# Hybrid encoder layer on one core: down weights of the short sequence split on GpSimd from the raw array instead of reloaded, loads reordered, a projection placed ahead of the first gates

## The reference

```python
proj = x @ w_in + b_in                                   # D_MODEL 1024 -> 7168
u_lru, g_lru, q, k, v, gate_lru, gate_attn = jnp.split(proj, SPLIT_IDX, axis=-1)
u = depthwise_conv(u_lru, w_lru_conv, b_lru_conv, LRU_CONV_PAD)
h_fwd = rg_lru_scan(u, ...)                              # gates: block-diagonal linear, 8 blocks of 160
h_bwd = flip(rg_lru_scan(flip(u), ...))
y_lru = ((h_fwd + h_bwd) * gelu(g_lru)) @ w_lru_out
attn = windowed_gqa(q, k, v, rel_table, attn_sink)       # keys within +-128
y_attn = attn @ w_attn_out
mix = (sigmoid(gate_lru) * y_lru + sigmoid(gate_attn) * y_attn) @ w_o + b_o
x = layer_norm(ALPHA * x + mix, ln1_g, ln1_b)
hu = depthwise_conv(x @ w_up + b_up, w_ffn_conv, b_ffn_conv, FFN_CONV_PAD)
val, gt = jnp.split(hu, 2, axis=-1)                      # D_FF 3072 each
ffn = (gelu(gt) * val) @ w_down + b_down
return layer_norm(ALPHA * x + ffn, ln2_g, ln2_b)
```

## Time and profile before

| | us |
|---|---|
| median of 3 runs | 2699.28 |
| lowest, highest | 2697.11, 2702.12 |
| the profiled execution | 2699.09 |
| span of its trace | 2697.2 |
| PE busy in it | 2608.7 |
| DVE, ACT, POOL busy | 1596.1, 956.7, 571.0 |

### The profile page before, as it was taken

How to read it: one execution, slowest core, us unless ns; L and a number is a source line. 1 busy time by engine, 2 the same in 40 slices (tenths; PEclk the granted TensorE clock), 3 DMA queues, 4 the chain that set the end, 5 groups by cost and what they waited for, 6 DMA issues and landing times.

```text
span 2697.2 us, 32662 instructions
## 1 busy us (share of the span) xinstructions
PE 2608.7 (97%) x11634; PEld 2150.2 (80%) x11634; DVE 1596.1 (59%) x2037; ACT 956.7 (35%) x1344; POOL 571.0 (21%) x306
## 2 busy tenths in 40 slices
PE   8999999999999999999999999989999999999998
PEld 6787888888788877788888778877788777888886
DVE  7799754334513658888888476457642424644445
ACT  3566713303400025444444333349732312111112
POOL 3554532232133612232322022300000000000000
PEclk9999999999999999999999999999999999999999
DMA  6555554544696843545354899966656783555554
GB/s 219 199 195 178 192 184 154 185 146 163 222 357 239 297 152 133 176 151 186 141 187 148 306 364 337 322 223 219 230 188 226 264 339 126 191 196 195 194 196 163
DMA packets 199872, 571.81 MB, mean 212 GB/s; under 512 B 16167, under 2 KB 43047, under 8 KB 197712
## 3 DMA queue, kind: packets, MB, share of 16 engines
q1 hardware_dynamic: 143712, 469.75, 48.4%
q10 hardware_dynamic: 56048, 100.59, 10.5%
HBM read 338.25 MB, written 223.10 MB: 208 GB/s over the span
## 4 chain that ended last, share of the span: by engine, by line
PE 81%; DVE 9%; DMA 5%; ACT 2%; issue 1%; ACTq 1%; POOL 0%; SPq 0%; DVEq 0%; POOLq 0%
PE ps L1177 35%; PE ps L1569 14%; PE ps L1345 9%; PE ps L1631 5%; PE ps L1519 5%; PE ps L1439 4%; PE ps L1227 3%; PE ps L1328 2%; PE ps L1378 2%; DMA gate_in<-gate_dram 1%; PE ps L1365 1%; PE ps L1230 1%; DMA Hd<-h_dram 1%; DMA W<-w_split 1%; DMA rest_raw<-w_up 1%
## 5 line engine op out<-in xcount | busy, mean ns | idle before, releaser
L1177 PE MATMUL ps<-XH,W 128*128 128x512 f32 x2752 | 812.1, 393 | 26.4 <-DVE XL L2371 11.8
L1177 PEld LDWEIGHTS ps<-XH,W 128*128 128x128 f32 x2752 | 519.3, 189 | 145.3 <-issue 19.1
L1177 PE MATMUL ps<-XL,W 128*128 128x512 f32 x1376 | 483.9, 391 | 0.0
L1177 PEld LDWEIGHTS ps<-XL,W 128*128 128x128 f32 x1376 | 260.3, 189 | 54.1
L1631 PE MATMUL ps<-Wd,Hd 128*128 128x512 f32 x1152 | 265.0, 392 | 8.4 <-DVE Hd L2883 8.4
L1631 PEld LDWEIGHTS ps<-Wd,Hd 128*128 128x128 f32 x1152 | 217.7, 189 | 55.6 <-DVE Hd L2883 10.2
L1345 PE MATMUL ps<-XH,W 128*128 128x512 f32 x672 | 216.4, 393 | 0.0
L1035 POOL TENSOR_SCALAR W<-raw 128x1024 fp32r<-128x1024 f32 (+2 forms) x72 | 90.3, 1254 | 563.1 <-PE ps L1177 302.5
L1036 POOL TENSOR_TENSOR W<-raw,W 128x1024 fp32r<-128x1024 f32 (+2 forms) x72 | 203.1, 2821 | 6.0
L1123 POOL TENSOR_TENSOR A<-raw,A 128x512 fp32r<-128x512 f32 x66 | 127.8, 1936 | 311.9 <-ACT A L2124 305.4
L1569 PE MATMUL ps<-XH,A 128*128 128x512 f32 x528 | 172.5, 394 | 4.9 <-ACT l_e L2148 2.6
(11 more groups left out here) (304 smaller groups left out, 4625.6 us busy)
## 6 DMA issues: line engine op xcount, KB each, us to landing
W<-w_split SPq DMA_DIRECT2D x130, 1024.0 KB, 6.6
w_split<-W SPq DMA_DIRECT2D x59, 1024.0 KB, 6.1
w_split<-A SPq DMA_DIRECT2D x66, 512.0 KB, 3.8
raw<-w_up SPq DMA_DIRECT2D x48, 512.0 KB, 5.8
raw<-w_down SPq DMA_DIRECT2D x48, 512.0 KB, 6.0
w_split<-Wd SPq DMA_DIRECT2D x24, 1024.0 KB, 7.6
raw<-w_qkv_mix SPq DMA_DIRECT2D x28, 512.0 KB, 4.0
h_dram<-l_h SPq DMA_DIRECT2D x24, 512.0 KB, 3.9
```

The source lines that it names most:

```text
L1177: last = nc.tensor.matmul(bank(group, c), lhs(wl, k), rhs(xl, k, c), start=(k == 0 and n == 0), stop=(k == nk - 1 and n == 2))
```

## The change

- **Short MLP.** The four down slabs of a group are no longer fetched as pairs. SP loads the raw slab from `w_down` (512 KB) into `raw[0]` and `raw[1]` by turns, POOL splits it into the slot, and PE waits for POOL (`rest_split`). A load into a buffer waits until the slab two before it is split. The loads stand behind the group's eight fetches in SP's order.
- **Long MLP, down product.** `save_down` and its 24 stores are gone, with the waits on them. The normed rows are loaded on every second step from step 4 to 18, the five bias and norm rows one at a time (steps 5, 6, 7, 13, 15), and the short sequence's x at steps 30 to 36, its heads at 38 to 45. DVE's adding of the normed rows moves accordingly.
- **Long MLP, start of the seven-product scheme.** ACT does `first_product(0, 0)` ahead of `plain_pair(1)`; DVE does `value_third(0, 0)` ahead of the last sums of pair 1; SP loads the raw slabs of the pair after that before it stores the forms.
- **lru, both sequences.** `("g", 0, 0)` stands ahead of `("gates", 0, 0)`, ACT takes its gelu before the gates, and in block 0 the own-channel matmuls of the first two (long) or four (short) groups are issued ahead of the wait for `u_stack`. The wait on `out_stored[1]` moves from before the first `u` to before that gelu.
- **Start.** x comes in parts of 1, 2, 3 and 2 slices, `cols` after all of x, and SP holds the second weight slab back until the second part of x is in, the third until all is.

```diff
-                     ("gates", 0, 0), ("g", 0, 0), ("u", 0, 2), ("g", 0, REST_TILE),
+                     ("g", 0, 0), ("gates", 0, 0), ("u", 0, 2), ("g", 0, REST_TILE),
...
+        X_PARTS = (0, 1, 3, 6, KD)
...
+                    if n in (1, 2):
+                        sp.wait_ge(x_landed[2 * n - 1], 16)
...
-                next_pair(2, 1, up_slab(3, 0))
+                sp.wait_ge(a_split, 6)
+                sp.wait_ge(form_added, 8)
+                load_pair(2 + PLAIN)
+                save_forms(1, 1, up_slab(3, 0))
+                store_h(1)
...
-                def save_down(s, slot, slab):
-                    sp.wait_ge(step_split, s + 1)
-                    sp.dma_start(w_split[slab, :, :, 0:D_MODEL], W_down[slot][:, :, :].bitcast(F32)).then_inc(w_saved[slot], 16)
...
-                    if s % 2 == 0:
-                        save_down(s - 2, (s - 2) % RING, down_slab(s - 2))
-                    else:
+                    if s % 2:
                         next_rest((s - RING) // 2)
...
+                def load_short_down(kk, g=0):
+                    if isinstance(g, int) and g == 0 and kk < 2:
+                        sp.wait_ge(out_stored[kk], 16 * out_count(0)[kk])
+                    else:
+                        sp.wait_ge(rest_split, FAST + FG * g + kk - 1)
+                    sp.dma_start(raw[kk % 2][:, 0:D_MODEL], A["w_down"][FG * g + kk, :, :]).then_inc(raw_in[kk % 2], 16)
+
-                for n in range(12):
+                for n in range(2 * FG):
...
                 with sp.Fori(0, NG - 1) as i:
-                    for n in range(12):
+                    for n in range(2 * FG):
                         fetch(s0 + 12 * i + n + 12 + 3 - slot_user(n), FIRST["mlp"] + 12 * i + n + 12, SLOT[n])
+                    for kk in range(FG):
+                        load_short_down(kk, i + 1)
...
+                with order.loop(NG, FG) as g:
+                    for kk in range(FG):
+                        k, n, slot = kk % 2, 2 * FG + kk, DOWN_SLOT[kk]
+                        pool.wait_ge(raw_in[k], 16 * RAW_SHORT + 32 * g + 16 * (kk // 2 + 1))
+                        pool.wait_ge(slab_done, s0 + 12 * g + n + 3 - slot_user(n))
+                        pool.sem_inc(begun, 1)
+                        order(pool.tensor_scalar(half(1, slot, 0)[:, 0:D_MODEL], raw[k][:, 0:D_MODEL], 1.0, 1.0, ALU.mult, ALU.mult))
+                        pool.tensor_tensor(half(1, slot, 1)[:, 0:D_MODEL], raw[k][:, 0:D_MODEL],
+                                           half(1, slot, 0)[:, 0:D_MODEL].bitcast(F32), ALU.subtract).then_inc(rest_split, 1)
...
+                        ahead = gate_banks(T) if blk == 0 else 0
+                        for place_of, m in enumerate(GATE_ORDER[0:ahead]):
+                            own_block(place_of, m)
+                        if q:
+                            pe.wait_ge(stack_in, 16 * (BLOCKS + blk + 1))
+                        pe.wait_ge(stack_moved[q], 48 * (blk + 1))
+                        for place_of, m in enumerate(GATE_ORDER + (4,)):
+                            if place_of >= ahead:
+                                own_block(place_of, m)
+                            rest_rows(place_of, m)
...
+                        first_product(0, 0)
                         plain_pair(1)
                         gate_centre(1)
                         value_centre(1)
-                        first_product(0, 0)
...
+                            if s == 5:
+                                act.wait_ge(h_ready, FT)
+                                act.wait_ge(h_stored, 16 * FT)
+                            if s % 2 == 0 and s < 4 + 2 * nt:
+                                load_normed((s - 4) // 2)
+                            if s in rows:
+                                dst, name, landed_rows = rows[s]
+                                act.dma_start(dst[:, :], A[name].partition_broadcast(P)).then_inc(landed_rows[0], 16)
...
+                                if s % 2 == 0 and s < FT + 6 + KD:
+                                    load_x(1, (s - FT - 6) // 2, (s - FT - 6) // 2 + 1)
+                                if FT + 14 <= s < FT + 14 + KD:
+                                    head_of_x(1, s - FT - 14)
```

More of the change, by code:

```diff
@@ L123 @@
         for _i in range(_n):
+            if _phase == "mlp" and _i % 12 >= 2 * FG:
+                continue
             _slot = slot_of(_q, _phase, _i)
@@ L131, in use @@
 def use(q, phase, n, g=0):
[L133 removed]
+    return USE[q][phase, n] + (UP_SLOT.count(SLOT[n]) * g if phase == "mlp" else 0)
 PLAIN = 2
@@ L1158, in _ @@
                 pool.sem_inc(cleared, 1)
+                s0 = first_slab(1, "mlp")
+                with order.loop(NG, FG) as g:
+                    for kk in range(FG):
+                        k, n, slot = kk % 2, 2 * FG + kk, DOWN_SLOT[kk]
[5 more added lines that the diff above has]
+                                           half(1, slot, 0)[:, 0:D_MODEL].bitcast(F32), ALU.subtract).then_inc(rest_split, 1)
+                        pool.wait_ge(rest_split, FAST + FG * g + kk + 1)
             @block.tensor
@@ L1184, in slab_in @@
                         pe.wait_ge(split_done, first_slab(q, phase) + n + 3)
+                    elif phase == "mlp" and n >= 2 * FG:
+                        pe.wait_ge(rest_split, FAST + FG * g + n - 2 * FG + 1)
                     else:
@@ L1211, in gates, with own_block @@
                         slab_in(q, "lru", n)
-                        if q:
-                            pe.wait_ge(stack_in, 16 * (BLOCKS + blk + 1))
-                        pe.wait_ge(u_split[q], channel_at[(h, jj)] + 1)
-                        pe.wait_ge(stack_moved[q], 48 * (blk + 1))
-                        if q == 0 and blk == 0:
-                            pe.wait_ge(consts_made, 2)
-                        for place_of, m in enumerate(GATE_ORDER + (4,)):
+                        w = [half(q, slot_of(q, "lru", n), t) for t in range(2)]
+                        ut = (u_head, u_tail)
+                        def own_block(place_of, m):
                             first = gate_bank(5 * blk + place_of, T)
                             pe.wait_ge(gate_evac[q], 5 * blk + place_of + 1)
-                            w = [half(q, slot_of(q, "lru", n), t) for t in range(2)]
-                            ut = (u_head, u_tail)
                             for i, (wl, xl) in enumerate(((0, 0), (0, 1), (1, 0))):
@@ L1812, in _ @@
                         act.wait_ge(consts_ready, 3)
+                    if q:
+                        act.wait_ge(out_stored[1], 16 * out_count(0)[1])
+                    take("g", 0, 0)
                     for h in range(2):
@@ L2313, in _ @@
                             act.wait_ge(out_stored[k], 16 * out_count(q)[k])
-                    if q == 0:
-                        for slot in range(2, 4):
-                            act.wait_ge(w_saved[slot], 16 * TOTAL[0][slot] + 16 * (FT // RING))
                     end_phase(act, end_of(q, "mlp"), wait=False)
@@ L2840, in first_period @@
                              t_split, 3)
+                        value_third(0, 0)
                         form_add(1, 1, "S3")
```

66 lines of the change are left out of this document (23 added, 43 removed).

## The result

| | us |
|---|---|
| before, median (4 runs beside the changed kernel) | 2698.52 |
| changed kernel, median of 4 runs (lowest, highest) | 2680.48 (2679.36, 2684.84) |
| ratio, with its 95% interval | 0.9934 (0.9917 to 0.9951) |
| its profiled execution, span | 2684.84, 2683.0 |

The change makes the kernel 0.66% faster. The median is 18 us lower.

What follows compares the result with a forecast made beforehand. PE was taken as the bound, busy 2608.7 of 2697.2 us, leaving 88.5 us of stalls and slow clock. Terms 0.5 + 1.3 + 4.6 + 10.4 + 9.4 - 3.5 = 22.7 us off 2699.1 gave 2676, range 2669 to 2689.

Steps and rivals of the forecast that it cites:

- 1 and 2, start and long lru: Start: smaller first part of x wins 0.5 us; long lru: gelu of `g 0 0` taken ahead wins 1.3.
- 3, first pairs of the scheme: Start of seven-product scheme: earlier raw slabs of pair 2 bring S3 forward 4.6 us, one stall replacing three.
- 4, long down product: Long MLP down product: without 24 stores and with x moved, three stalls and lower clock go, 10.4 us won.
- 5, long to short: First short gates: moved projection and own-channel matmuls cover the 6.85 us wait and end the slow clock, 9.4 us won.
- 6, GpSimd's splits: Short MLP down slabs: splits on time in five groups, late in the last, 3.5 us lost.
- term 2: Long lru order: the 1.32 us gelu wait goes, 1.3 us won; slack falls to about 1 us; bounds -1 and +1.3.
- Rival (b): Short MLP: DVE and POOL hinder each other, first split 1 to 2 us late in every group; centre 2686; chance 0.11.
- (a): Long down product still stalls at step 6 through another wait, up to 8 of 10.4 us lost; 2686; chance 0.14.
- (c): Slower: SP's queue in the short MLP waits for POOL, six groups take 32 us; from 2705 us; chance 0.05.
- (d): Whole kernel: nothing measurable, (a) and half of rival (b) at once; 2694 to 2700 us; chance 0.04.
- my likeliest case: Whole kernel: the summed terms hold, 2676 us, own range 2670 to 2683; chance 0.66.
- One sign of being wrong: Long lru: a PE stall behind the second long gates would show the slack of term 2 was missing; no size given.

Runs made afterwards that it cites:

- again: The changed kernel measured a second time with no edit; median 2680.76 us, ratio 0.994.
- start_firsts_back: Changed kernel with x in four equal parts, old SP holds, and first product and value third of pair 0 in their old places; 2680.44 us.
- load_order_back: Changed kernel with the raw slabs of pair 2 loaded behind the stores of forms again; 2684.55 us.
- last_saved: Changed kernel, but the last short group's four down slabs are split and stored by the long sequence and fetched as pairs; 2675.13 us, ratio 0.9918.

## Why the prediction was right, point by point

The forecast of 2676 was 4.5 us low, inside its range. Added up stage by stage, the measured terms give 18.2 us (changed) and 17.8 (`again`), which is the 18.0 between the medians; I had 22.7. The terms fared less evenly than the sum:

| term | predicted us | changed, `again` |
|---|---|---|
| 1 and 2, start and long lru | 1.8 | -0.2, -0.5 |
| 3, first pairs of the scheme | 4.6 | 2.9, 2.9 |
| 4, long down product | 10.4 | 12.1, 12.1 |
| 5, long to short | 9.4 | 9.0, 9.0, of which 5.2 and 8.8 were left at the short attention |
| 6, GpSimd's splits | -3.5 | -5.6, -5.7 from the first short down product on |

**Start and long lru.** The start was right: PE begins 0.83 us earlier, I had 0.5, and start_firsts_back shows 0.65 us of it still there at 238 us. The new order (term 2) was mis-sized, 1.3 us for a loss, and the step that failed was to take the stall at the gelu alone. The 1.32 us there went. But the stall in the first gates is 1.35 us and was 0.70, 0.69 us came behind the second gates, and the stall at 238 us grew from 6.57 to 6.92. PE comes out of that one at 238.33, 0.17 us earlier than before, of which the start is 0.65: the new order costs 0.5 us. The wait of 0.69 us is the one that term 2 named, for the PSUM of `u 0 2`, with "a slack of about 1 us" that was not there. The lower bound of the term, -1, was nearer than my value.

**The scheme.** The mechanism, the landing of pair 2's slabs, was right (load_order_back), but its worth was mis-sized: S3 begins 3.3 us earlier and not 4.6. I expected one stall of about 5 us in place of three; there are three again, 1.70, 1.37 and 5.11, 0.4 us less in all than the 8.55 of before. The rest of the 2.9 us is matmuls that run faster: the granted clock is 0.93 in 1060 to 1110 after 0.90. That the two calculations help was not borne out: the one trace without them is 1.5 us shorter there (start_firsts_back).

**The down product** gained 12.1 us, more than the 10.4 that I had set as its upper bound. A fourth stall stood in the trace of before and not in my sum:

```profile
1563.95 81.93 PE L1631 MATMUL ps<-Wd,Hd 128*128 128x512 f32 x360 [0.69 <-DVE Hd L2883]
```

The four stalls are 8.4 us, and so the slow matmuls behind them 3.7 and not 2.7. The reason was only half right. I took the traffic and ACT's four issues as two causes that the change both removes. Either alone costs 1.0 us or less; it is their meeting, with the rows on top.

**Long to short.** Right to 0.4 us at the second gates. That some of it went afterwards in one profile and little in the other is more likely chance of the execution than the change: the kernel before has the stall of 1840 us too (1.75 us, at 1862.79), and what differs is its clock and length from one execution to the next.

**The splits.** A POOL split took 1.15 + 2.62 us on the mean here, with its gaps what I had (4.1). In the last group slab 3 was split 12.06 us after PE began slab 0 (11.9 by my sum), and PE's three stalls add to 3.67 us, within the 3 to 4 that I named. And yet the term was larger: 4.5 to 4.6 us in that group, as last_saved shows. What I left out is that DVE's chain to the last `HL` is held up by the same instructions, 0.46 us, and what PE loses around each stall besides the stall (4.63 against 3.67 us). The other 1.0 and 1.3 us were lost before it. Rival (b) had the mechanism of POOL and DVE hindering each other, but put its price in every group. In the first five PE reaches the fourth slab, which needs that `HL`, some 16 us after the first (three times 5.44), in the last group after 8.

**The rivals.** (a), (c) and (d) did not come. The time lies between my likeliest case and (b), and (b)'s mechanism is in it with about half a us, at one place in six. Of the signs that I named, the full clock and the absence of stalls at steps 6 to 12, the stall of 4 to 6 us before S3 and the stalls of the last group came; at the first short gates 0.47 us are left. One sign of being wrong came as well, the stall behind the second long gates.

## What to carry to other kernels

Price a piece of work moved to GpSimd twice: by its own length on the path, and by what DVE's chain loses while it runs, and look for the place where the consumer has no slack, here the last group, where the first price was 4 us and the second half a us. The cheapest mend is to leave only that place as it was: four stores kept of 24 made the fastest version. Before adding up stalls, ask what each later wait hangs on; a stall removed in a loop whose loads depend on another engine's chain comes back further on.

## What was not expected of the hardware

- A DVE instruction that begins while a POOL one runs ended 0.54 to 0.55 us after the POOL one in three cases, 2.01 to 2.75 us long instead of 0.69 to 0.75. In the short MLP's groups DVE's `HL` took 1072 ns on the mean instead of 693.
- Full DMA queues (0.97 of the time, 367 GB/s) did not stop PE; full queues and a burst of 2 MB more, in four issues of 256 to 768 KB, did, for 9 us. A slab of 512 KB behind that burst took 13 us to land.
- The same 24 matmuls took 7.38 or 5.74 us, behind a stall of 2.00 or 1.73 us, with a granted clock of 0.83 or 1.00 over those 10 us; in another run a stall of 2.07 us there left the clock at 1.00.
